# Layer 0's expert rows added in memory by accumulating indirect DMAs instead of by matrix products

## The reference, cut to what matters

```
aff = softmax(h @ w_router);  top_w, top_idx = top_k(aff.T, cap)        # cap = 64 latent, 32 context
xg  = h[top_idx]
hid = silu(xg @ w_gate) * (xg @ w_up)
ye  = (hid @ w_down) * top_w
out = zeros.at[top_idx].add(ye)          # a row may be picked by several experts, or by none
x   = x + mod[5] * out
```

## Time and profile before

| | |
|---|---|
| median of 3 runs | 2638.04 us |
| the profiled execution's own time | 2638.16 us |
| its span, first to last instruction | 2636.4 us |
| PE busy | 2481.1 us, 94% of the span |
| DVE / ACT / POOL busy | 1055.8 / 680.8 / 87.6 us |
| mean granted clock of TensorE | 0.987 |
| bytes moved by DMA | 580.72 MB, 220 GB/s over the span |

### The profile page before, as it was taken

The page is one execution under the profiler, slowest core; times in us unless marked ns, Lnnn a source line. Parts: engine busy times, 40 slices in busy tenths (PEclk is TensorE's granted clock), DMA queues, the critical chain, the costliest instruction groups (busy, mean ns, idle before and its releaser), DMA issues. The chain is left out here.

```text
span 2636.4 us, 41046 instructions
## 1 busy us (share of the span) xinstructions
PE 2481.1 (94%) x17556; PEld 1568.7 (60%) x17556; DVE 1055.8 (40%) x2307; ACT 680.8 (26%) x1348; POOL 87.6 (3%) x145
## 2 busy tenths in 40 slices
PE   5999999999899899999999999999999999999998
PEld 3888877778686444454444588876677643333432
DVE  4545354344774313223231664445348431111113
ACT  3621232222633111121111362143236311010101
POOL 1000100000000000000100000100000000000000
PEclk9999999999999999999999999999999999999999
DMA  6111556151553999897989211322216379999996
GB/s 217 57 49 33 141 197 202 62 167 47 196 174 117 384 363 392 308 394 299 383 331 366 101 48 62 77 86 73 72 57 207 134 286 410 409 409 409 409 409 276
DMA packets 241827, 580.72 MB, mean 220 GB/s; under 512 B 11462, under 2 KB 120240, under 8 KB 240624
## 3 DMA queue, kind: packets, MB, share of 16 engines
q1 hardware_dynamic: 232160, 550.21, 55.9%
q0 software_dynamic: 9488, 27.90, 3.3%
HBM read 554.94 MB, written 23.13 MB: 219 GB/s over the span
## 5 line engine op out<-in xcount | busy, mean ns | idle before, releaser
L1042 PE MATMUL ps<-h_hi,m_lo 128*128 128x512 f32 (+1 forms) x1152 | 347.2, 373 | 2.0 <-DVE arena L2263 1.7
L1483 PE MATMUL ps<-arena 128*32 128x512 f32 x1740 | 259.2, 593 | 1.7 <-ACT arena L1925 1.3
L1484 PE MATMUL ps<-arena 128*32 128x512 f32 x588 | 258.0, 593 | 0.0
L1015 PE MATMUL ps<-m_lo,h_hi 128*128 128x256 f32 (+1 forms) x1248 | 236.1, 291 | 5.1 <-DVE m_lo L2236 2.9
L1042 PEld LDWEIGHTS ps<-h_hi,m_lo 128*128 128x128 f32 x1152 | 208.7, 190 | 52.3 <-issue 13.7
L1015 PEld LDWEIGHTS ps<-m_lo,h_hi 128*128 128x128 f32 x1248 | 198.6, 197 | 13.7 <-issue 9.7
L1042 PE MATMUL ps<-h_lo,m_lo 128*128 128x512 f32 (+1 forms) x576 | 205.6, 357 | 0.0
L1629 PE MATMUL ps<-arena 128*64 128x512 f32 x832 | 187.8, 597 | 11.6 <-DMA arena<-in_moe_w_up 8.9
L1015 PE MATMUL ps<-m_lo,h_lo 128*128 128x256 f32 (+1 forms) x624 | 178.6, 286 | 0.0
L1483 PEld LDWEIGHTS ps<-arena 128*32 128x32 f32 x1740 | 70.3, 110 | 164.3 <-issue 160.8
L1015 PE MATMUL ps<-h_hi,m_lo 128*128 128x512 f32 (+1 forms) x512 | 141.9, 354 | 7.8 <-DVE h_lo L2341 6.9
(11 more groups left out here) (407 smaller groups left out, 4499.4 us busy)
## 6 DMA issues: line engine op xcount, KB each, us to landing
arena<-in_moe_w_up SPq DMA_DIRECT2D x101, 1024.0 KB, 11.4
arena<-in_moe_w_gate SPq DMA_DIRECT2D x100, 1024.0 KB, 11.7
arena<-in_moe_w_down SPq DMA_DIRECT2D x100, 1024.0 KB, 13.2
ring<-in_w_in SPq DMA_DIRECT2D x42, 1024.0 KB, 5.3
arena<-in_ada_w SPq DMA_DIRECT2D x37, 1024.0 KB, 5.9
oT<-in_moe_w_up SPq DMA_DIRECT2D x27, 1024.0 KB, 14.7
oT<-in_moe_w_down SPq DMA_DIRECT2D x24, 1024.0 KB, 8.9
oT<-in_moe_w_gate SPq DMA_DIRECT2D x16, 1024.0 KB, 8.6
```

What stands on the lines that cost most here:

```text
L1015: last = mm(to, stationary, moving, start=at == 0 and k == 0, stop=at == 2 and k == KD - 1)
L1042: last = mm(to, w[:, k, cols], h[:, k, seg], start=n == 0 and k == 0, stop=n == 2 and k == KD - 1)
L1483: mm(ps[r][32 * b:32 * b + 32, :], c_xg[:, k, j, 32 * b:32 * b + 32], w, start=k == 0, stop=k == KD - 1)
L1484: last = mm(ps[r][96:128, :], c_xg[:, k, j, 32 * r:32 * r + 32], up[:, kk, 512:1024], start=k == 0, stop=k == KD - 1)
```

## The change

In layer 0 nothing is scattered by PE any more. Once the routing is done, SP copies the residual's six tiles to a buffer in memory, `x_acc`, behind the first 11 weight loads. DVE takes an expert's 96 rows out of PSUM with gate and weight in one instruction (`scalar_tensor_tensor`) into a buffer of its own per expert of the turn. POOL adds each finished expert to `x_acc` by one accumulating indirect DMA of 96 rows of 4 KB; each waits for the one before it (two experts may hit one row). After the sixteenth, SP loads the six tiles back into `x_sb`, each with a semaphore of its own, and ACT squares a tile when it has landed. Layer 1 loads its residual later from `x_acc`; `x_spill` and its stores are gone.

```
-        SCATTER_AT = {(0, 2): (0, 1), (0, 3): (2, 3, 4, 5), (1, 0): (6, 7, 8), (1, 1): (9, 10, 11)}
...
+                    sp.wait_ge(scattered, 16 * E)
+                    for t in range(NT):
+                        sp.dma_start(x_sb[:, t, :], x_acc[t * P:(t + 1) * P, :]).then_inc(x_back(t)[0], 16)
...
+                    if l == 0 and n == SLOTS_OF[l]:
+                        for t in range(NT):
+                            sp.dma_start(x_acc[t * P:(t + 1) * P, :], x_sb[:, t, :]).then_inc(x_kept, 16)
...
+            def rows_added(g, j):
+                pool.wait_ge(ye_ok, g * 8 + 2 * j + 2)
+                if g or j:
+                    pool.wait_ge(scattered, 16 * (GE * g + j))
+                nc.gpsimd.indirect_dma_start(x_acc, bass.IndirectOffsetOnAxis(slot_row(g, j)[0:ROWS, :], 0), ye[j][0:ROWS, :], None,
+                                             compute_op=ALU.add).then_inc(scattered, 16)
...
-                        for q in () if first else SCATTER_AT.get((j, kp), ()):
-                            scatter(g - 1, q)
-                        if (j, kp) == (1, 2):
-                            pe.wait_ge(hidT_act, before("hidT_act", l) + g * 8 + 2)
-                            selection_turned(g, first)
...
                 if l:
-                    kept_running(ps[0], 3)
+                    kept_running(ps[0], 24)
...
                 kept_running(ps[0], 7)
-                for q in range(nq):
-                    scatter(TURNS - 1, q)
...
+                    kept(slice(64, 96), slice(768, 1024), rest[other, 0:256], (other, 2, 512))
+                    kept(own, slice(0, 512), first_half[own, :], (own, 0, 0)).then_inc(ye_ok, 1)
+                    kept(own, slice(512, 768), second_half[own, 0:256], (own, 0, 512))
+                    kept(slice(0, 32), slice(768, 1024), second_half[other, 0:256], (other, 0, 768))
+                    kept(slice(32, 64), slice(768, 1024), first_half[other, 0:256], (other, 1, 768)).then_inc(ye_ok, 1)
```

More of the change, by code:

```diff
@@ L614, in slot_bank, with slot_row, x_back, slot_landings @@
             return 5 if g else 5 + p
[L616 to L620, removed]
-        SCATTER_AT = {(0, 2): (0, 1), (0, 3): (2, 3, 4, 5), (1, 0): (6, 7, 8), (1, 1): (9, 10, 11)}
-        def moe_done(l):
-            return E // GE * 2 * NQ[l]
+        def slot_row(g, j):
+            at = 3 + GE * (g % 2) + j
+            return row_at[:, at:at + 1]
+        def x_back(ti):
+            return pair_in[ti], 16 * slot_landings(DEPTH - 1, ti)
+        def slot_landings(l, slot):
+            loads = sum(len(range(slot, TURNS * PER_TURN, slots)) for slots in SLOTS_OF[:l] if slot < slots)
+            return loads + max(1, LATE_SLOTS.count(slot)) + (1 if l and slot < NT else 0)
         def slot_count(l, j, slots):
@@ L1462, in pair_arrived @@
                 slot = n % SLOTS_OF[l]
-                earlier = sum(len(range(slot, TURNS * PER_TURN, slots)) for slots in SLOTS_OF[:l] if slot < slots)
-                pe.wait_ge(pair_in[slot], 16 * (earlier + max(1, LATE_SLOTS.count(slot))) + 16 * (n // SLOTS_OF[l] + 1))
+                pe.wait_ge(pair_in[slot], 16 * (slot_landings(l, slot) + n // SLOTS_OF[l] + 1))
             def experts_in_groups(l):
-                nq = 2 * NQ[l]
                 GATHER_AT = ((0, 1), (2, 3), (4, 5), (6, 7))
@@ L1950, in results_high @@
-                def results_high(g, pieces):
-                    act.wait_ge(weights_ok, 2 * g + 2)
-                    for p, half in pieces:
-                        act.wait_ge(ye_ok, before("ye_ok", l) + g * 8 + (4 if p == 0 else 7 + half))
-                        do(ye_hi[p][half], ye_part(p)[0][:, 512 * half:512 * half + 512], ACT.Copy, scale=slot_w[:, p:p + 1]
-                           ).then_inc(ye_hi_ok, 1)
+                    act.wait_ge(row_at_ok, 4 * g + 4)
+                    if g >= 2:
+                        act.wait_ge(ye_ok, before("ye_ok", l) + (g - 1) * 8)
@@ L2464, in results, with kept @@
-                    v.tensor_tensor(lat[r + 32:r + 64, 768:1024], first_half[96:128, 0:256], gate5[96:128, 768:1024], ALU.mult).then_inc(ye_ok, 1)
+                    def kept(rows, cols, part, gate):
+                        r, c, n = gate
+                        return v.scalar_tensor_tensor(y[rows, cols], part, w[r, c:c + 1], gate5[r, n:n + cols.stop - cols.start], ALU.mult, ALU.mult)
+                    own, other = slice(0, ROWS), slice(96, 128)
+                    kept(slice(64, 96), slice(768, 1024), rest[other, 0:256], (other, 2, 512))
@@ L2536, in grouped @@
                 turn(TURNS - 1, False, True)
[L2537 to L2540 removed]
+                for ti in range(NT):
+                    normed_behind(2 * l + 2, ti)
                 normed_last(2 * l + 2)
```

163 lines of the change are left out of this document (57 added, 106 removed).

## The result

The changed kernel takes 2617.27 us (median of 5 runs, 2615.39 to 2627.82) against 2645.73 us for the kernel before, timed beside it (5 runs, 2634.02 to 2646.74). The ratio is 0.9916, with a 95% interval of 0.9895 to 0.9936: 0.8% faster, or 22 us (17 to 28), since the ratio goes by all runs and not by the medians, which lie 28 us apart. The forecast was 2617.7 us, 20.5 us less than before. One time of the kernel before, 3927.67 us with a granted clock of 0.594 (beside experiments 7 and 8), is left out of every comparison.

A forecast was written before the change was run, and what follows sets the result against it. PE was taken to bound layer 0's experts. Products removed gain 28.3 us, less 4.8 for lost cover and 3.0 at the experts' end: 20.5 us off 2638.2, so 2617.7 us, range 2608 to 2640.

The forecast's parts named there:

- What bounds the kernel: Layer 0's experts are bound by PE, so work leaving PE there shortens the program until the loads become the bound.
- Products that go: Layer 0's scatter products and one-hot transposes leave PE, with a wait for first results: gain 28.3 us.
- (1, 0), (1, 1): Two places in a turn of layer 0's experts with 12 scatter products each, 6.36 us together.
- the 12 products at (0, 3): Ahead of expert 0's transposes in layer 0: only cover for PE's wait for ACT and DVE; removal worth 0.12 us.
- Lost cover: PE idles 4.7 us without filler in turns 1 to 3; the clock falls, costing 1.6 us each, 4.8 us.
- DVE and ACT: More casts and copies ahead of expert 2's silu cost nothing, with about 1 us to spare.
- DMA: Four accumulates in a turn of layer 0 have 3.7 us each, take 2 us; the loads stay ahead of PE.
- Rival A: Accumulates make layer 0's loads the bound: no change (2630 to 2638), chance 0.11, or slower (2651 us), 0.13.
- The end of the experts: Behind layer 0's last expert, PE's 31 fillers are the bound; first projection at T + 30.6, cost 3.0 us.
- Rival B: Last accumulate and way back behind layer 0's experts take 9 us beyond the room: 2627 us, chance 0.14.
- C: Clock holds through the 4.7 us idles: 2613 us; a variant within the forecast's 0.62.
- D: Change takes nothing off the path, as the cover was all PE did there; held for 12 of 40 products only.

The follow-up runs named there:

- experiment 7: Changed kernel with 19, or 3, instead of 24 filler products ahead of layer 1's first transposes: 2615.99 us (ratio 0.9906) and 2623.1 us (0.9923).
- experiment 8: Changed kernel with fillers wherever PE waits over 2 us around the experts: 2610.68 us (ratio 0.9884); also with 19 tail fillers instead of 24: 2605.26 us (0.9857).
- experiment 3: Kernel before, without 18 of the 24 scatter products at (1, 0) and (1, 1) in the first three turns' scatters: 2635.6 us, ratio 0.9964.
- the best one: Changed kernel with fillers wherever PE waits over 2 us around the experts, and 19 instead of 24 fillers ahead of layer 1: 2605.26 us, ratio 0.9857.
- experiment 2: Kernel before, without 8 of the 12 scatter products ahead of expert 0's transposes in the first three turns' scatters: 2649.55 us, ratio 1.002.
- experiment 1: The changed kernel run once more, unchanged: 2620.19 us, ratio 0.9918 to the kernel before.
- experiment 4: Changed kernel with each of the first 15 accumulates sent again into arrays nothing reads: twice as many 2624.55 us, four times 2679.17 us.
- experiment 6: Three filler products ahead of the router's last transposes: in the changed kernel 2619.81 us (ratio 0.9917), in the kernel before 2635.07 us (0.9975).

## Why the prediction was right, step by step

**The number.** That 2617.27 stands beside 2617.7 is in part luck. The forecast was 20.5 us less than 2638.2; timed beside the changed kernel the one before had a median of 2645.73. By the ratio the change is worth 22 us (17 to 28), by the two profiles with the short stretch 16.9, with the same fillers in both kernels 15. The stages that the change touches give 20.5 us in the first profile (23.5 - 3.0) and 18.5 in the second.

**What bounds the kernel.** Right: experiment 3 shows that products in the open are on the path, the legs below that all of them together are worth their time, and neither the changed kernel nor the best one waits for weights in layer 0.

**Products that go: forecast 28.3 us, measured 30.3.** The kernel of experiment 8 has the change without the clock's falls: 526.16 us from the first transposes to T, against 556.5 before. By place: the leg with (1, 0), (1, 1) and the one-hot transposes fell from 39.78 to 31.90 us, 7.9 where I had 7.6, three times; turn 0's by 1.38 instead of 1.24; the leg that ends at expert 0's transposes by 1.83 instead of 1.41 (4 products, 0.12 and a wait of 0.23), three times. Each place is some tenths larger than its products' durations. One tenth a place is the interruption itself: the last gate or up product before a group starts 0.52 us ahead of it (1087.33 to 1087.85), where such steps follow each other every 0.43. What makes the rest is not known. That the 12 products at (0, 3) were only cover, the step on which 9.2 us of the sum hung, is shown by experiment 2 and by the waits: 4.64 us, where 4.7 was forecast.

**Lost cover: forecast 4.8 us, measured 6.9.** The changed kernel's four distances less those of experiment 8 are 0.2, 2.1, 3.0 and 1.6. I had priced a fall at 1.6 us from the earlier trace rows, 3.2 us at the lower level. The rule behind it, half of the time that PE runs at 1.2 GHz, was right; that time was 3.4 to 6.2 us here, so a fall costs 1.6 to 3.0. The three legs of experiment 1 less those of experiment 8 are 1.6, 2.6 and 3.1, 7.3 us in all. This term and the one above erred by 2 us each, in opposite directions. Their sum came out at -23.5 us in the first profile, as forecast, and at -21.5 in the second; that it did so exactly is luck.

**DVE and ACT.** Nothing, as forecast: no wait of PE ahead of expert 2's transposes, and its leg (35.4 to 35.6 us in the first profile, 35.3 to 35.5 before) is what it was. In experiment 1 it is 35.8 to 36.2 us, with 0.4 us of PE's idle that nothing in the trace ended; why is open.

**DMA.** The assumed 2 us an accumulate is measured at 1.9 to 2.0 (experiment 4). The room of 3.7 us was real too: at twice the accumulates the loads just begin to be felt. Rival A would have needed the accumulates to be 2.5 times as dear as they are.

**The end of the experts.** Fillers end at T + 26.8 (forecast 27.2), first projection at T + 30.65 (30.6), the accumulate lands in 5.6 us (5), the data are ready at T + 22.8 (21.1). Of these 1.7 us, DVE and the hand-over to POOL took 0.4, the accumulate 0.6, the way back and the scaling the rest. Cost 3.0 us, as forecast; experiment 7 shows whose it was. Rival B, the longer chain, had 4.0 us to go.

**Rivals C and D.** The clock did not hold. D's part of truth, cover at one place in four, is the lesson of experiment 2.

**What I did not foresee** is the stretch ahead of the experts: one execution may lose 11 us there, as much as half of what the change gives. A single profile does not hide it, and the median of a few runs does not either: that of the unchanged kernel was 2638.04 in three runs and 2645.73 in five.

## What to carry to other kernels

Price a removed instruction by its place, not its duration: eight products that stood in a wait were worth less than nothing (their removal let the clock fall, 1.7 us a time), equal ones elsewhere were worth most of their time, and all of it once they were all gone. Look at the legs between two fixed points of a trace before the span: the span of one run held 11 us that the change had not made. And when a change uncovers waits, put filler work there in the same step; with it, and with the tail of fillers cut to the data's arrival, the kernel came out 1.4% (37 us) below the one before instead of 0.8% (22). Some 7 of these 15 us may come from the stretch ahead, which the kernel before can have as well (experiment 6).

## What the runs showed of the hardware

- The same wait of 3.0 us on PE was followed by a return of the clock to 2.4 GHz within 4 us in one execution, and by some 31 us at 1.2 GHz in another, of the same kernel, though PE was busy for 28.9 of 30.5 us of them. Three of the ten profiles without a filler in that wait have the long stretch. In these three the clock fell 0.9 to 1.1 us before PE went on, in the other seven 0.2 to 0.7 us before; that this decides it is not shown. In the four profiles with three fillers there it did not occur, and the clock fell for 3.4 to 10 us behind the next wait, of 2.65 us.
- Behind the 4.64 us waits, in dense expert work, the clock was back 3.5 to 6.4 us behind the wait's end (profiles of the changed kernel and of experiment 1), and 4.5 us behind the 14 us wait at the tail.
- A wait of 2.35 us in dense work was enough for a fall (0.50 from 1068 to 1070 us, some 2 us behind the wait's end); waits of 1.01 and 1.21 us at the same place were not.
- An accumulating indirect DMA of 96 rows, 0.393 MB, held the engines for 2.0 us, took POOL 1.42 us to issue, and landed in 5.6 us alone and 8.6 among weight loads; the added ones of four times as many landed in 11.3.
